# Queue orders of the mixing stage: sample scores at chunks 4 and 8, at mix's end and in retention, and queries times past states with sides swapped

## The chip, the cores and the metric

The kernel runs on 1 core of one Trainium2 chip. The metric is the device time of one execution in microseconds, and lower is better. A core has TensorE (PE in the profile), VectorE (DVE), ScalarE (ACT), GpSimd (POOL) and SyncE (SP), which here only issues DMAs. Engines are ordered among each other by semaphores alone; each runs its own instructions strictly in the order in which they are written.

## The reference, cut to what matters

The program is one inference step of a 2-layer decoder. Each layer has a feed-forward part, a mixing part and a second feed-forward part, over 256 prompt tokens and 8 sample sequences of 8 tokens each (320 columns in all).

```python
x = x + 0.5 * swiglu(rmsnorm(x, g_ffn1), f1_in, f1_out)
z = rmsnorm(x, g_mix) @ w_in
u, qa, ka, va, qr, kr, vr, gr = jnp.split(z, offs, axis=-1)
y_pool, pool_new = pool_mixer(u, pool_prefix, pos, pool_w, pool_scale)
y_att = ...   # per sequence: softmax over its own keys, and for samples over 8 cached pages of 128 keys
o_r, ret_new = retention(qr, kr * HEAD_DIM ** -0.5, vr, ret_s0)
y_ret = silu(gr) * o_r * rsqrt(mean(o_r ** 2) + EPS)
x = x + concat([y_pool, y_att, y_ret]) @ w_out
x = x + 0.5 * swiglu(rmsnorm(x, g_ffn2), f2_in, f2_out)
```

Retention of a sample adds the product of its queries, decayed, with its past state (a 64x64 matrix per head and sequence): `o = att @ v + (q * q_dec) @ s`.

## The kernel before

Every weight matrix streams from HBM in chunks of 256 columns (1 MB). SP loads a chunk into `w_raw` (two slots), ACT rounds it to `w_hi` (`hi_split`, L587), DVE forms the rest `w_lo` (`lo_split`, L844), and PE multiplies three times (L1235 to L1237 in the feed-forward parts, L1317 to L1319 in mixing). PE can start a chunk only when its `w_lo` is there.

The change lies in the mixing part of both layers, the body of the loop over `L` after the first feed-forward part. There each engine has an order of work that is written out by hand:

- PE runs `mix(0)` to `mix(11)`, the twelve chunks of `w_in`. `mix(c)` needs chunk c split and the first half of chunk c-1 evacuated (`evac_first(c-1)`, L933, which counts `mix_half`). Between chunks stand pieces of attention: `scores(f)` and `transpose_p(h)` and `att_out(f)` for the prompt; `sample_scores(p)` for pair p of the 8 sample sequences (p = 0 to 3); `past_states()`, the queries times the past states. Then come retention (`ret_scores`, `ret_out`, `smp_state`), the softmax results times the cached values (`smp_out`), and the output projection (`out_part`).
- `sample_scores(p)` multiplies the queries with 16 pages of keys: 8 pages in `kbuf[0]` and 8 in `kbuf[1]`. DVE must have turned them in place (`turn_k`, L990, half a buffer each). `key_scores` counts `sc_done` when it is done with a buffer.
- SP loads weight chunks (`mix_load(c)`) and pages (`next_k(p, bb)`: waits for `sc_done`, then issues 8 page loads of 192 KB). All these go through SP's one queue, in the order of the code. `mix_load(c)` also waits until chunk c-2 is split.
- DVE runs `evac_first`, `evac_last`, `mix_lo(c)` (a `lo_split`), `turn_k`, the prompt's softmax (`smax(h)`, `normalise(h)`), and the samples' (`soft_in(p)` reads the scores from PSUM, `soft_bias(p)` selects blocks and finds maxima, `soft_sum(p)` adds). ACT runs `mix_hi(c)` (a `hi_split`), the copies of turned tokens (`ka_tokens`, `va_tokens`), and the exponentials (`exp(h)`, `exps(p)`).
- POOL does the pooling sums, prepares queries (`qprep(p)`) and loads the pages of values (`load_v`).

Before the change `sample_scores(0)` stands ahead of `mix(6)`, (1) ahead of `mix(10)`, (2) after `ret_scores(1)` and (3) after the mean squares; SP has pages of pair 1 after chunk 8 and those of pair 2 after chunk 11. The scores of pair 3 use pair 0's buffer `sp_a` again.

`past_states` multiplies, for each of 3 pairs of heads, a stationary 128x128 block of states with 16 columns of queries at a time:

```python
pe.matmul(ps[:, 3, P * f + c:P * f + c + 2 * NT], s0[:, f, b:b + 2, :].rearrange("p b v -> p (b v)"),
          q[:, c:c + 2 * NT], start=True, stop=True)
```

Of the kernel before, what the change touches and what calls it, by code (L numbers as in the profile page):

```python
# [108 lines left out]
def build(nc, A, C, O):  # L109
# [8 lines left out]
    with ctx:  # L118
# [181 lines left out]
        def _(sp_e):  # L300
# [137 lines left out]
        def _(pool):  # L438
# [37 lines left out]
            with pool.Fori(0, DEPTH) as L:  # L476
# [26 lines left out]
                for n, w in enumerate(WINDOWS):  # L503
# [78 lines left out]
        def _(act):  # L582
# [63 lines left out]
            with act.Fori(0, DEPTH) as L:  # L646
# [20 lines left out]
                def va_tokens(t):  # L667
# [119 lines left out]
                act.wait_ge(stored_u, 32 * (L + 1))  # L787
                for f in range(3):
# [5 lines left out]
                exps(2)  # L794
# [921 lines left out]
```

## Time and profile before

| | us |
|---|---|
| median of 3 runs | 1453.36 (1450.92 to 1453.76) |
| the profiled execution's own time | 1445.9 |
| its span | 1443.9 |
| PE busy | 1360.1 (94%) |
| DVE busy | 812.1 (56%) |
| ACT busy | 650.0 (45%) |
| POOL busy | 216.7 (15%) |

The mixing part of the first layer lies between about 262 and 478 us of the span, that of the second between about 965 and 1179 us. In the trace a matmul's bar is longer than its share of the engine, since matmuls overlap; the distance from start to start tells what one takes. "[x <-Y]" at a row's end says that the engine was idle for x us before it, and what ended that.

### The profile page before, as it was taken

The numbers are of one execution on the slowest core, as the hardware profiler recorded it, in microseconds if no ns is written. First come the engines' busy times: TensorE is split into PE (matmuls) and PEld (weight loads), VectorE is DVE, ScalarE is ACT, GpSimd is POOL, SyncE is SP. The second block draws the span as 40 slices with busy tenths as digits, with TensorE's granted clock in tenths as the row PEclk, the third lists the DMA queues.
The fourth block names the chain that finished last, engine by engine and source line by source line (L and its number), as shares of the span: only waits on it lengthen the run. The fifth ranks groups of instructions, "written<-read, shape, count | busy, mean of one in ns | idle before, by whom it ended". The sixth has DMA issues, their size and how long they took to land.

```text
span 1443.9 us, 28417 instructions
## 1 busy us (share of the span) xinstructions
PE 1360.1 (94%) x11165; PEld 1306.2 (90%) x11165; DVE 812.1 (56%) x870; ACT 650.0 (45%) x715; POOL 216.7 (15%) x343
## 2 busy tenths in 40 slices
PE   6999999899877999999999999989997789999998
PEld 4999999899656899999999999989984579999998
DVE  4655545477673665554455555456867546555454
ACT  4655533334223565553355554432434245555433
POOL 3000001370334100000100000034313611000001
PEclk9999999999988999999999999999999899999998
DMA  6444445753758344444444444475637744444443
GB/s 207 150 145 145 143 160 180 209 166 115 219 179 277 118 145 146 151 152 144 152 142 156 152 145 135 158 236 142 208 110 221 258 153 146 145 145 145 142 153 121
DMA packets 210895, 235.27 MB, mean 163 GB/s; under 512 B 14974, under 2 KB 203144, under 8 KB 210804
## 3 DMA queue, kind: packets, MB, share of 16 engines
q1 hardware_dynamic: 200828, 204.90, 43.8%
q0 software_dynamic: 9856, 29.14, 6.4%
q8 instruction: 55, 0.90, 0.3%
q14 instruction: 36, 0.29, 0.1%
q10 hardware_dynamic: 120, 0.03, 0.0%
HBM read 228.83 MB, written 5.32 MB: 162 GB/s over the span
## 4 chain that ended last, share of the span: by engine, by line
PE 84%; issue 7%; DVE 5%; DVEq 1%; POOLq 1%; DMA 1%; ACT 1%; POOL 0%; SPq 0%; ACTq 0%
PE ps L1235 21%; PE ps L1237 21%; PE ps L1236 21%; PE ps L1317 4%; PE ps L1319 4%; PE ps L1318 4%; PE ps L1457 2%; DVE kbuf L990 1%; PE ps L1495 1%; PE ps L1402 1%; DVEq L1165 1%; PE ps L1630 1%; DVE h_lo L851 0%; DVE w_lo L844 0%; DMA x_tok<-in_x_sample 0%
## 5 line engine op out<-in xcount | busy, mean ns | idle before, releaser
L587 ACT ACTIVATE w_hi<-w_raw 128x2048 fp32r<-128x2048 f32 x170 | 325.6, 1915 | 554.6 <-PE ps L1237 427.3
L844 DVE TENSOR_TENSOR w_lo<-w_raw,w_hi 128x2048 fp32r<-128x2048 f32 x170 | 391.4, 2303 | 210.4 <-ACT w_hi L587 207.7
L1235 PE MATMUL ps<-h_hi,w_hi 128*128 128x320 f32 x768 | 241.0, 314 | 9.5 <-DVE w_lo L844 3.5
L1236 PE MATMUL ps<-h_lo,w_hi 128*128 128x320 f32 x768 | 239.7, 312 | 0.0
L1237 PE MATMUL ps<-h_hi,w_lo 128*128 128x320 f32 x768 | 239.5, 312 | 0.0
L1235 PE MATMUL ps<-g_hi,w_hi 128*128 128x320 f32 x704 | 218.4, 310 | 1.2 <-DVE g_lo L851 1.2
L1237 PE MATMUL ps<-g_hi,w_lo 128*128 128x320 f32 x704 | 217.7, 309 | 0.0
L1236 PE MATMUL ps<-g_lo,w_hi 128*128 128x320 f32 x704 | 217.7, 309 | 0.0
L1236 PE MATMUL ps<-act_lo,w_hi 128*128 128x320 f32 x704 | 217.5, 309 | 0.0
L1235 PE MATMUL ps<-act_hi,w_hi 128*128 128x320 f32 x704 | 217.5, 309 | 0.0
L1237 PE MATMUL ps<-act_hi,w_lo 128*128 128x320 f32 x704 | 217.5, 309 | 0.0
L1235 PEld LDWEIGHTS ps<-h_hi,w_hi 128*128 128x128 f32 x768 | 146.2, 190 | 11.4 <-issue 5.9
L1236 PEld LDWEIGHTS ps<-h_lo,w_hi 128*128 128x128 f32 x768 | 146.3, 191 | 0.2
L1237 PEld LDWEIGHTS ps<-h_hi,w_lo 128*128 128x128 f32 x768 | 146.3, 191 | 0.0
L1235 PEld LDWEIGHTS ps<-g_hi,w_hi 128*128 128x128 f32 x704 | 132.2, 188 | 1.9 <-DVE g_lo L851 1.7
L1236 PEld LDWEIGHTS ps<-g_lo,w_hi 128*128 128x128 f32 x704 | 132.2, 188 | 0.2
L1237 PEld LDWEIGHTS ps<-g_hi,w_lo 128*128 128x128 f32 x704 | 132.2, 188 | 0.0
L1236 PEld LDWEIGHTS ps<-act_lo,w_hi 128*128 128x128 f32 x704 | 132.2, 188 | 0.0
L1237 PEld LDWEIGHTS ps<-act_hi,w_lo 128*128 128x128 f32 x704 | 132.2, 188 | 0.0
L1235 PEld LDWEIGHTS ps<-act_hi,w_hi 128*128 128x128 f32 x704 | 132.2, 188 | 0.0
L1317 PE MATMUL ps<-h_hi,w_hi 128*128 128x320 f32 x368 | 119.2, 324 | 8.1 <-DVE z L933 6.9
L449 POOL COPY ssq<-tmp 128x640 f32<-128x640 f32 x7 | 8.0, 1147 | 751.9 <-ACT tmp L612 751.9
(275 smaller groups left out, 1923.4 us busy)
## 6 DMA issues: line engine op xcount, KB each, us to landing
w_raw<-in_ffn_w_in SPq DMA_DIRECT2D x90, 1024.0 KB, 5.1
w_raw<-in_ffn_w_out SPq DMA_DIRECT2D x32, 896.0 KB, 4.6
kbuf<-in_cache_k SPq DMA_DIRECT2D x128, 192.0 KB, 3.3
w_raw<-in_w_in SPq DMA_DIRECT2D x22, 1024.0 KB, 5.7
w_raw<-in_ffn_w_out SPq DMA_DIRECT2D x16, 1024.0 KB, 5.0
kbuf<-in_cache_v POOLq DMA_DIRECT2D x64, 192.0 KB, 4.4
w_raw<-in_w_out SPq DMA_DIRECT2D x8, 1024.0 KB, 7.5
v_c<-in_cache_v POOLq DMA_DIRECT2D x32, 192.0 KB, 3.4
```

Of the source, the lines that this page charges most:

```text
L587: act.activation(w_hi[:, slot, :], w_raw[:, slot, :], ACT.Copy).then_inc(hi_done, 1)
L844: dve.tensor_tensor(w_lo[:, slot, :], w_raw[:, slot, :], w_hi[:, slot, :].bitcast(F32), ALU.subtract).then_inc(split_done, 1)
L990: dve.transpose(keys, keys).then_inc(kt_ok, 1)
L1165: dve.drain()
L1235: pe.matmul(out, w_hi[:, slot, w], hi[:, k, :], start=(k == 0), stop=False)
L1236: pe.matmul(out, w_hi[:, slot, w], lo[:, k, :], start=False, stop=False)
L1237: ins = pe.matmul(out, w_lo[:, slot, w], hi[:, k, :], start=False, stop=(k == k_all - 1))
L1317: pe.matmul(out, w_hi[:, c % 2, w], h_hi[:, k, :], start=(k == 0), stop=False)
L1318: pe.matmul(out, w_hi[:, c % 2, w], h_lo[:, k, :], start=False, stop=False)
L1319: ins = pe.matmul(out, w_lo[:, c % 2, w], h_hi[:, k, :], start=False, stop=(k == KT - 1))
L1402: pe.matmul(ps[:, 3, P * f + c:P * f + c + 2 * NT], s0[:, f, b:b + 2, :].rearrange("p b v -> p (b v)"), q[:, c:c + 2 * NT], start=True, st ...
L1457: ins = pe.matmul(ps[32 * f:32 * f + 32, 2 + r, 0:256], q_sc[p][R, bb, f, a, j, :], kbuf[bb][R, :, c:c + 32], start=(bb == 0 and n == 0), ...
```

## The change

1. PE: `sample_scores(0)` moves ahead of `mix(5)`, `sample_scores(1)` ahead of `mix(9)`, `sample_scores(2)` ahead of the later tokens of retention, `sample_scores(3)` ahead of the last `smp_state`; `scores`, `transpose_p` and `tokens` move by about one chunk the other way. `out_part(0, early)` moves behind `smp_out(2, 1)`.
2. SP: pages of pair 1 are loaded ahead of chunk 7, those of pair 2 ahead of chunk 10.
3. DVE and ACT: their orders follow. `turn_k` of pair 0 starts at chunk 0.
4. A buffer of its own for the scores of pair 3 (`sp_d`, in `w_lo`'s first slot), so `mix_lo(12)` now waits for all transposes of probabilities.
5. `past_states`: queries are the stationary side (32 columns), states the moving side (128 columns): 12 matmuls a layer in place of 27 (three times nine). The result lies by query rows, and `ret_out` turns it with two matmuls per head in place of one.

```diff
@@ block.sync
-                for c in range(3, 8):
+                for c in range(3, 7):
                     mix_load(c)
+                next_k(1, 0)
+                next_k(1, 1)
+                mix_load(7)
                 sp_e.wait_ge(u_out, 2 * L + 2)
...
                 mix_load(8)
-                next_k(1, 0)
                 sp_e.wait_ge(ka_out, 3 * L + 2)
                 store_kv(0, "k", ka_tok, None, stored_k)
-                next_k(1, 1)
                 mix_load(9)
+                next_k(2, 0)
+                next_k(2, 1)
+                mix_load(10)
                 sp_e.wait_ge(va_out, 3 * L + 2)
                 store_kv(0, "v", va_tok, None, stored_va)
-                mix_load(10)
                 mix_load(11)
-                next_k(2, 0)
-                next_k(2, 1)
@@ block.scalar
                 mix_hi(7)
                 ka_tokens(1)
+                exps(0)
                 exp(0)
                 exp(1)
                 mix_hi(8)
                 va_tokens(0)
+                mix_hi(9)
+                va_tokens(1)
                 probs_out(0)
                 probs_out(1)
                 exp(2)
                 exp(3)
-                mix_hi(9)
-                va_tokens(1)
-                exps(0)
                 mix_hi(10)
                 att_evac(0)
+                exps(1)
+                mix_hi(11)
+                ka_tokens(2)
                 probs_out(2)
                 probs_out(3)
...
@@ block.vector
                 evac_first(4)
-                turn_k(0, 1, 0)
                 evac_last(4)
+                mix_lo(6)
+                soft_in(0)
+                evac_first(5)
+                soft_bias(0)
+                evac_last(5)
+                mix_lo(7)
                 smax(0)
                 dve.drain()
                 smax(1)
-                mix_lo(6)
-                evac_first(5)
...
-                evac_last(7)
+                evac_last(8)
+                mix_lo(10)
                 normalise(2)
                 normalise(3)
-                mix_lo(9)
                 soft_sum(0)
-                turn_k(1, 0, 0)
-                evac_first(8)
-                turn_k(1, 0, 1)
-                evac_last(8)
+                dve.wait_ge(pool_d, L + 1)
+                soft_in(1)
+                evac_first(9)
+                soft_bias(1)
+                evac_last(9)
+                mix_lo(11)
                 smax(4)
                 dve.drain()
                 smax(5)
-                mix_lo(10)
...
+                evac_first(10)
+                turn_k(2, 0, 0)
+                evac_last(10)
+                turn_k(2, 0, 1)
                 dve.wait_ge(past_done, L + 1)
...
                 y_rest(0)
                 for f in range(3):
                     or_lo(f)
+                y_rest(1)
+                dve.wait_ge(pt2_done, NB * L + 8)
                 mix_lo(12)
@@ block.tensor
                     for f in range(3):
                         q = q_dec[:, f, :, :, :].rearrange("p b a t -> p (b a t)")
-                        pe.matmul(ps[HD:P, 3, P * f:P * f + NT], s0[:, f, 0, :], q[:, 0:NT], start=True, stop=True)
-                        for b in range(NB - 1):
...
+                        for g in range(4):
+                            ins = pe.matmul(ps[32 * g:32 * g + 32, 3, P * f:P * f + P], q[:, 32 * g:32 * g + 32],
+                                            s0[:, f, 2 * g:2 * g + 2, :].rearrange("p b v -> p (b v)"), start=True, stop=True)
...
                 u_tokens()
-                scores(0)
                 tokens(ZKA, 0, 7).then_inc(ka_tr, 1)
+                pe.wait_ge(kown_ok, L + 1)
+                sample_scores(0)
                 mix(5)
...
                 tokens(ZKA, 1, 7).then_inc(ka_tr, 1)
+                wait_apart(pe, sm_in, L * 4 + 1)
+                scores(0)
                 mix(6)
...
                 tokens(ZVA, 0, 7).then_inc(va_tr, 1)
-                transpose_p(0)
-                transpose_p(1)
-                scores(1)
                 mix(7)
                 pe.wait_ge(va_out, 3 * L + 1)
                 tokens(ZVA, 1, 7).then_inc(va_tr, 1)
+                transpose_p(0)
+                transpose_p(1)
+                wait_apart(pe, s_max, H * L + 2)
+                scores(1)
                 mix(8)
                 pe.wait_ge(va_out, 3 * L + 2)
                 att_out(0)
...
+                pe.wait_ge(s_max, H * L + 4)
+                sample_scores(1)
                 mix(9)
                 wait_apart(pe, oa_out, 3 * L + 1)
                 tokens(ZKA, 2, 7).then_inc(ka_tr, 1)
+                transpose_p(2)
+                transpose_p(3)
+                scores(2)
+                past_states()
                 mix(10)
                 pe.wait_ge(ka_out, 3 * L + 3)
                 att_out(1)
+                wait_apart(pe, past_ok, L + 1)
+                tokens(ZVA, 2, 3).then_inc(va_tr, 1)
+                mix(11)
```

Three places of the new orders follow, as the built programs have them.

SP's queue at the load of chunk 7, before (chunks 6 and 7, then the stores of `u_tok`):

```order
L305 DMA w_raw<-in_w_in 128x8x256
L303 ISA
L305 ISA
L305 DMA w_raw<-in_w_in 128x8x256
L303 REGISTER_ALU
L305 ISA
L305 DMA w_raw<-in_w_in 128x8x256
L376 ISA
L377 ISA
L377 DMA out_pool_prompt<-u_tok 15x256
```

and after the change (the last page of the 16 of pair 1, then chunk 7; `kbuf_60` is `kbuf[1]`):

```order
L358 ISA
L358 DMA kbuf_60<-in_cache_k 128x384
L304 REGISTER_ALU
L306 ISA
L306 DMA w_raw<-in_w_in 128x8x256
L380 ISA
L381 ISA
L381 DMA out_pool_prompt<-u_tok 15x256
```

The 16 page loads of pair 1, which wait for the scores of pair 0, now stand ahead of chunk 7.

DVE at the split of chunk 7, before (`smax(0)`'s end and `smax(1)`, chunk 6, `evac_first(5)`, `turn_k`, `evac_last(5)`, chunk 7; L933 is `evac_first`, L938 `evac_last`):

```order
L949 SCALAR_TENSOR_TENSOR s_p<-dist_p,ps 128x384
L952 TENSOR_REDUCE st<-s_p 128x1
L953 TENSOR_REDUCE st<-s_p 128x1
L955 TENSOR_SCALAR st<-st 128x2
L843 ISA
L844 TENSOR_TENSOR w_lo<-w_raw,w_hi 128x2048
L932 REGISTER_ALU
L933 TENSOR_TENSOR z<-ps,rstd 128x320
L990 STREAM_TRANSPOSE kbuf_60<-kbuf_60 128x1536
L936 REGISTER_ALU
L938 TENSOR_TENSOR z<-ps,rstd 128x320
L843 REGISTER_ALU
```

and after (chunk 7's split L847, then `smax(0)` and `smax(1)`, then `evac_first(6)` L936):

```order
L847 TENSOR_TENSOR w_lo<-w_raw,w_hi 128x2048
L948 ISA
L952 SCALAR_TENSOR_TENSOR s_p<-dist_p,ps 128x384
L955 TENSOR_REDUCE st<-s_p 128x1
L956 TENSOR_REDUCE st<-s_p 128x1
L958 TENSOR_SCALAR st<-st 128x2
L948 REGISTER_ALU
L952 SCALAR_TENSOR_TENSOR s_p<-dist_p,ps 128x384
L955 TENSOR_REDUCE st<-s_p 128x1
L956 TENSOR_REDUCE st<-s_p 128x1
L958 TENSOR_SCALAR st<-st 128x2
L935 REGISTER_ALU
```

`smax(0)` and `smax(1)` stood ahead of the splits of chunks 6 and 7, and stand behind that of chunk 7 now, ahead of `evac_first(6)`.

DVE after `evac_first(8)`, after the change (the end of `q_dec`, `evac_last(8)`, chunk 10's split, `normalise(2)`, `normalise(3)`):

```order
L1098 TENSOR_TENSOR q_dec<-z,q_decay 64x8x8 x6
L939 REGISTER_ALU
L941 TENSOR_TENSOR z<-ps,rstd 128x320
L846 ISA
L847 TENSOR_TENSOR w_lo<-w_raw,w_hi 128x2048
L963 RECIPROCAL st<-st 128x2
L965 TENSOR_SCALAR s_p<-s_p,st 128x256
L966 TENSOR_SCALAR s_p<-s_p,st 128x128
L963 RECIPROCAL st<-st 128x2
L965 TENSOR_SCALAR s_p<-s_p,st 128x256
L966 TENSOR_SCALAR s_p<-s_p,st 128x128
```

Before, `normalise(2)` and `normalise(3)` followed `evac_last(7)` at once and stood ahead of chunk 9's split; now they stand behind chunk 10's.

## Rows read from the trace of the kernel before

**Rows 1.** Busy time by stretches: start:end, length, PE, PEld, DVE, ACT, POOL, PEclk, DMA share, GB/s

```profile
640.00:680.00 40.00, 40.00 (x275) 40.00 (x274) 19.45 (x14) 15.79 (x12) 1.21 (x1) 1.00 0.45 145
400.00:440.00 40.00, 25.18 (x401) 16.81 (x400) 28.43 (x56) 11.15 (x29) 17.39 (x36) 0.78 0.63 195
```

**Rows 2.** PE in order of time (start us, us), first layer: chunks 7, 8, 10, 11; the projection

```profile
325.06 0.42 PE L1317 MATMUL ps<-h_hi,w_hi 128*128 128x320 f32 x1
332.44 0.39 PE L1317 MATMUL ps<-h_hi,w_hi 128*128 128x320 f32 x1
365.64 0.41 PE L1317 MATMUL ps<-h_hi,w_hi 128*128 128x320 f32 x1
374.31 0.39 PE L1317 MATMUL ps<-h_hi,w_hi 128*128 128x320 f32 x1
...
439.19 0.65 PE L1503 MATMUL ps<-ident,o_tok 96*128 96x96 f32 x2 [7.35 <-ACT o_tok L720]
...
470.88 0.41 PE L1630 MATMUL ps<-h_hi,w_hi 128*128 128x320 f32 x1 [0.97 <-DVE h_lo L1177]
```

**Rows 3.** In order of time: the end of chunk 4 (DVE's last evacuation), the scores of pair 0 (PE)

```profile
302.39 0.49 DVE L938 TENSOR_TENSOR z<-ps,rstd 128x320 f32<-128x320 f32 x1 [0.47 <-PE ps L1319]
...
311.42 4.28 PE L1457 MATMUL ps<-kbuf,q_sc_a 32*32 32x256 f32 x192
```

**Rows 4.** SP's queue in order of time, first layer

```profile
314.61 5.04 SPq L357 DMA_DIRECT2D kbuf<-in_cache_k  x8
...
321.09 5.50 SPq L357 DMA_DIRECT2D kbuf<-in_cache_k  x8
326.84 0.38 SPq L305 DMA_DIRECT2D w_raw<-in_w_in  x1
...
362.99 10.46 SPq L357 DMA_DIRECT2D kbuf<-in_cache_k  x16
```

**Rows 5.** DMA issues of 326.8:327.3, then of 284:286: KB each, us to landing

```profile
w_raw<-in_w_in SPq DMA_DIRECT2D x1, 1024.0 KB, 7.8
...
w_raw<-in_w_in SPq DMA_DIRECT2D x1, 1024.0 KB, 5.3
```

**Rows 6.** The page's groups by line: the two halves of a split (busy us, mean ns)

```profile
L587 ACT ACTIVATE w_hi<-w_raw 128x2048 fp32r<-128x2048 f32 x170 | 325.6, 1915 | 554.6 <-PE ps L1237 427.3
L844 DVE TENSOR_TENSOR w_lo<-w_raw,w_hi 128x2048 fp32r<-128x2048 f32 x170 | 391.4, 2303 | 210.4 <-ACT w_hi L587 207.7
```

**Rows 7.** DVE in order of time: two `smax`; then `soft_in(0)`, `evac_first`, `soft_bias(0)`, `evac_last`

```profile
303.67 0.56 DVE L949 SCALAR_TENSOR_TENSOR s_p<-dist_p,ps 128x384 f32<-128x384 f32 x1 [0.79 <-PE ps L1367]
307.03 2.28 DVE L844 TENSOR_TENSOR w_lo<-w_raw,w_hi 128x2048 fp32r<-128x2048 f32 x1
...
317.79 1.22 DVE L997 TENSOR_REDUCE ss<-ps 96x4 f32<-96x1024 f32 x1 [0.18 <-issue]
320.63 0.49 DVE L933 TENSOR_TENSOR z<-ps,rstd 128x320 f32<-128x320 f32 x1 [0.17 <-issue]
...
324.56 0.48 DVE L938 TENSOR_TENSOR z<-ps,rstd 128x320 f32<-128x320 f32 x1
```

**Rows 8.** PE in order of time: `past_states` begins, chunk 9 begins behind it; a piece of `smp_out`

```profile
342.12 0.28 PE L1399 MATMUL ps<-q_dec,s 128*64 128x8 f32 x2
...
348.26 0.64 PE L1317 MATMUL ps<-h_hi,w_hi 128*128 128x320 f32 x1
...
453.64 1.95 PE L1495 MATMUL ps<-v_d,pt_s 128*32 128x128 f32 x48
```

**Rows 9.** Stretches, columns as in rows 1: chunk 9 behind `past_states`, PE around and after its longest wait

```profile
349.00:354.00 5.00, 5.00 (x20) 5.00 (x20) 1.98 (x2) 0.00 (x0) 0.00 (x0) 0.50 0.00 0
436.00:446.00 10.00, 5.60 (x68) 4.51 (x71) 5.17 (x8) 6.89 (x21) 6.85 (x13) 0.51 0.99 347
```

**Rows 10.** PE in order of time: the scores of pair 3, first and second buffer

```profile
416.49 3.56 PE L1457 MATMUL ps<-kbuf,tmp 32*32 32x256 f32 x96 [3.38 <-DVE kbuf L990]
422.43 3.84 PE L1457 MATMUL ps<-kbuf,tmp 32*32 32x256 f32 x96 [2.39 <-DVE kbuf L990]
```

More of the change, by code:

```diff
@@ L755, in _ @@
                 exp(5)
-                mix_hi(11)
-                ka_tokens(2)
+                att_evac(1)
                 va_tokens(2)
-                att_evac(1)
                 probs_out(4)
                 probs_out(5)
-                exps(1)
                 act.wait_ge(stored_va, 16 * (L + 1))
@@ L793, in _ @@
                     root_o(f)
-                exps(2)
                 probs_evac(0)
-                for f in range(3):
-                    or_high(f)
+                exps(3)
                 out_evac(0, 0)
@@ L800, in _ @@
                 probs_evac(1)
+                for f in range(3):
+                    or_high(f)
                 y_high(0)
-                exps(3)
-                mix_hi(12)
                 out_evac(1, 0)
@@ L1066, in _ @@
                 smax(1)
-                mix_lo(6)
-                evac_first(5)
-                turn_k(0, 1, 1)
-                evac_last(5)
-                mix_lo(7)
+                evac_first(6)
+                turn_k(1, 0, 0)
+                evac_last(6)
+                mix_lo(8)
                 normalise(0)
                 normalise(1)
-                soft_in(0)
-                evac_first(6)
-                soft_bias(0)
-                evac_last(6)
+                turn_k(1, 0, 1)
+                evac_first(7)
+                turn_k(1, 1, 0)
+                evac_last(7)
+                mix_lo(9)
+                turn_k(1, 1, 1)
                 smax(2)
@@ L1080, in _ @@
                 smax(3)
-                mix_lo(8)
-                evac_first(7)
+                evac_first(8)
                 dve.memset(q_dec[:], 0.0)
@@ L1104, in _ @@
                 smax(5)
[L1105 to L1109 removed]
+                evac_first(10)
+                turn_k(2, 0, 0)
+                evac_last(10)
+                turn_k(2, 0, 1)
                 dve.wait_ge(past_done, L + 1)
[L1111 to L1114 removed]
+                for half in range(2):
+                    ins = dve.tensor_copy(o_past[half][:], ps[:, 3, 0:384].rearrange("p (f b v) -> p f b v", f=3, b=2)[:, :, half, :])
                 ins.then_inc(past_ok, 1)
[L1116 removed]
                 normalise(4)
                 normalise(5)
[L1119 to L1125 removed]
+                evac_last(11)
+                turn_k(2, 1, 0)
+                turn_k(2, 1, 1)
+                soft_sum(1)
+                dve.wait_ge(chunk_used, L * C_ALL + (C_MIX + 14))
+                soft_in(2)
                 dve.wait_ge(stored_k, 32 * (L + 1))
@@ L1137, in _ @@
                 k_tokens(2)
-                turn_k(2, 1, 0)
-                turn_k(2, 1, 1)
                 decay_mask(1)
+                soft_bias(2)
+                turn_k(3, 0, 0)
                 for t in range(2):
@@ L1149, in _ @@
                 decay_mask(3)
+                turn_k(3, 0, 1)
                 gate(0)
-                soft_in(2)
+                decay_mask(4)
+                turn_k(3, 1, 0)
                 new_state(0)
-                decay_mask(4)
+                decay_mask(5)
+                turn_k(3, 1, 1)
                 gate(1)
                 new_state(1)
-                decay_mask(5)
                 gate(2)
+                soft_in(3)
                 new_state(2)
-                soft_sum(1)
-                soft_bias(2)
+                soft_sum(2)
+                soft_bias(3)
                 def or_norm(f):
@@ L1178, in y_rest @@
                     ins.then_inc(ys_low, 1)
-                for half in range(2):
-                    turn_k(3, 0, half)
-                or_norm(0)
-                for half in range(2):
-                    turn_k(3, 1, half)
-                soft_in(3)
-                soft_sum(2)
-                soft_bias(3)
-                or_norm(1)
-                or_norm(2)
+                for f in range(3):
+                    or_norm(f)
                 y_rest(0)
@@ L1647, in _ @@
                 transpose_out(2)
+                chunk_split(half0 + C_WO // 2, 0)
+                wait_apart(pe, o_std, 3 * L + 3)
+                pe.wait_ge(att_low, L + 1)
+                pe.wait_ge(ret_low, 3 * L + 3)
+                out_part(0, early, True)
                 smp_out(3, 0)
```

107 lines of the change are left out of this document (37 added, 70 removed).

## Prediction

> **What bounds the kernel now.** I read the table of busy time by stretches first, then PE in order of time through the mixing part of the first layer, then SP's queue and DVE's order at the places where PE would wait. In the feed-forward parts PE is busy for all of a 40 us stretch [rows 1], so the change can neither gain nor lose there. In the mixing part PE has holes: 25.2 of 40 us busy between 400 and 440, at a granted clock of 0.78 [rows 1]. The longest wait is 7.35 us, for ACT's `o_tok`, the longest of the waits for keys is 3.4 us [rows 2, 10]. Up to chunk 11, though, the chunks follow each other nearly without a hole, 7.4 us apiece (332.44 less 325.06) [rows 2]. So PE is the bound up to there, with DVE, ACT and the weight chunks ahead of it by some microseconds, and in the tail PE, DVE and ACT wait in turn. The same order of work runs in both layers; I work out one and double it.
>
> **The change part by part.**
>
> *Where pair 0 is scored.* Chunk 4 ends at 302.4 [rows 3]. Then come some 0.7 us of turned tokens and, now, `sample_scores(0)`. Its queries, its keys and its own keys are prepared in time: POOL's first pooling step now starts some 1 us after DVE's copy of the prefix and is followed by `qprep(0)`, and the four `turn_k` of 1.8 us each stand in places where DVE waited for PE. I take nothing for them; if they were late, the scores and all behind them would shift by as much as the 1.8 us of one `turn_k`. So the scores run from 303.1 to 307.7: 4.3 us, and 0.4 for the own keys [rows 3]. This is only a move; chunk 5 starts later and chunk 6 at about 316.4, as before within half a microsecond.
>
> *Chunk 7 behind 16 pages.* This is the term that decides. Half of the scores free `kbuf[0]`, at 305.3. In the trace SP's first page went out 1.0 us after that point (314.61 against 311.42 + 2.1) [rows 3, 4], so now at 306.3. Sixteen pages take SP 10.5 us to issue [rows 4]: 316.8. Chunk 7 is issued 0.3 us later, at 317.1. A chunk lands 5.3 us after its issue on an empty queue, and 7.8 behind 16 pages [rows 5]; I take 6.5, in the middle, with both as ends: 323.6. ACT's half of the split is 1.9 us and DVE's 2.3 [rows 6], with 0.1 for each hand-over: 327.9. Behind it on DVE stand `smax(0)` and `smax(1)`, 3.3 us together (303.67 to 307.03 [rows 7]), since the change put them behind the split, and only then `evac_first(6)`, 0.5, for which `mix(7)` waits: 331.7. PE is ready at 324.1 and idles for over 7 us. Chunk 7 started at 325.1 before [rows 2], so 6.6 us are lost (5.4 to 7.9 by the two landings).
>
> *To the scores of pair 1.* Chunk 7 is 7.4 us; its tokens, `transpose_p(0)`, `transpose_p(1)` and `scores(1)`, 2.0 in all, now follow it: `mix(8)` at 341.1, against 332.4 [rows 2]. It ends at 348.5, `att_out(0)` takes 0.8, and then PE waits for `smax(3)`, which I find at 350.2 by adding up DVE's order from `evac_first(6)` on. So `sample_scores(1)` begins at 350.2.
>
> *Chunk 10 behind 16 pages.* The same once more, and worse. `kbuf[0]` is free at 352.6, the pages go out from 353.0 to 363.5 [rows 4], chunk 10 at 363.8, landing at 370.3 (369.1 to 371.6) [rows 5], split at 374.7 [rows 6]. PE has done with chunk 9 at about 362.3 and then needs `att_evac(0)`, which stands behind `mix_hi(10)` on ACT, and `normalise(2)`, `normalise(3)` and `soft_in(1)`, which stand behind `mix_lo(10)` on DVE: 1.8, 0.4 for `soft_sum(0)`, and 2.8 (317.79 to 320.63 [rows 7]): 379.7. Then 0.4 for `transpose_p(3)`, 0.9 for `scores(2)`, and `past_states`: `mix(10)` begins at 382.0 against 365.6 [rows 2].
>
> *`past_states` with sides swapped.* Before, it takes 6.1 us (342.12 to 348.26) [rows 8] and leaves PE at the lower of its two clock levels: 0.50 of 2.4 GHz over 349 to 354, 20 records in 5 us [rows 9] where chunk 7 has 48 in 7.4, so 1.8 us lost in that stretch, 2.7 over all that runs slowly. The new form is nearest to `smp_out`, also 32 stationary and 128 moving columns: 48 records in 1.9 us [rows 8], 39 ns each. The 12 matmuls make 24 records, 0.9 us; even at the old 6.1 us it would be no loss. A gain of 5.2, 7.9 with the clock, is already in the 382.0 above. The extra matmul per head in `ret_out` adds under 0.2 us three times.
>
> The Trainium skill, TensorE: Matmul & The Clock Gate, section Back-to-back issue gap, puts a stream of weight loads and matmuls of 128 columns at about 81 ns each. By that `past_states` would take 1.9 us (an estimate from the page: 24 records), and the layer's sum would stay, since DVE sets the next step; the row's 39 ns speaks for less.
>
> *To chunk 11.* DVE goes on from 379.7: `evac_first(9)` 0.5, `soft_bias(1)` 3.6, `evac_last(9)` 0.4 (the last two by [rows 7]): 384.2. `mix_hi(11)` stands on ACT behind `exps(1)` (2.5): 388.6, `mix_lo(11)` 390.9, `smax(4)`, `smax(5)` 394.3, `evac_first(10)`, two `turn_k`, `evac_last(10)` 4.5: 398.8, and the copies of `o_past`, 0.7. The tokens that chunk 11 stands behind wait for these, since they use their bank. `mix(11)` begins at 399.9, against 374.3 [rows 2]: 25.6 us late.
>
> *The tail.* For: the waits of 3.4 and 2.4 us for the keys of pair 3 go [rows 10], since `sp_d` and the earlier place give these time. Against: `mix_lo(12)` may start only after the last transposes of probabilities, so its 2.3 us show ahead of `out_part(0)`; and `exps(3)`, `soft_bias(3)` and the three reciprocals now stand close together where PE waited 7.35 us [rows 2]. I find 2.5 us gained from `mix(11)` to the last parts of the projection; ends are 10 gained (both waits for keys and half of the 7.35) and 3 lost.
>
> *The clock.* PE's wait of 7.35 us was followed by the lower level: 0.51 over 436 to 446 [rows 9]. Three waits of 7, 16 and 9 us are new; the slow stretches after `past_states` and at the scores of pair 3 go. I take the two as equal, with 7 us more per layer as the upper end.
>
> *Sum.* 25.6 - 2.5 = 23.1 us per layer, some 46.5 in all. The profiled execution, 1445.9 us by its own time with a span of 1443.9, would be about 1492. The median of the runs stands 7.5 above it, so the median comes to 1453.4 + 46.6 = **1500 us**.
>
> **The rivals.**
>
> *Rival 1: the chunks are late, but the tail gives most of it back.* What is done later in the middle is done while the tail's other work catches up; the tail has some 20 us of idle PE and a low clock [rows 1, 2, 10]. Against it: the tail's waits are on DVE and ACT chains that cannot start before retention. It would leave some 8 to 12 us per layer: 1469 to 1477, say 1474.
>
> *Rival 2, the other side: the chunks are in time.* The kernel then gains. Place: chunk 7's and chunk 10's splits. It decides at 324 for chunk 7 and at about 364 for chunk 10: if pages and chunk together land 4 us sooner for the first, and 11 sooner for the second, PE never waits. Then `past_states` gives 7.9 us and the tail 2.5 to 4: 11 per layer, 1431. Against it stand the issue time of 16 pages, seen at 10.5 us without anything in between, and the landing of the chunk behind them [rows 4, 5].
>
> *Rival 3: the clock costs more.* Every long wait is followed by up to 8 us at 1.2 GHz, as after 439 [rows 2, 9], and none of it hides: 7 us more per layer, 1514. The Trainium skill, TensorE: Matmul & The Clock Gate, section What's actually happening, has the low clock as the default that only activity lifts; by it this rival holds at each of the three waits. Against it: after them DVE, not PE, sets the next step.
>
> *Rival 4: the change does not do what it says.* The fourth home lets `soft_in(3)` run early, but nobody waits for it if the values' pages or the reciprocals come last. It is inside the tail's range.
>
> **How the numbers follow.** Late chunks with the tail as worked out, 0.62 (1500, its own range 1486 to 1511); rival 3, 0.13 (1514); rival 1, 0.16 (1474); rival 2, 0.07 (1431); chunks partly late so that gain and loss cancel, 0.02. The range of 1470 to 1520 leaves out rival 2 and the edges of 1 and 3. A measurement of this kernel can tell about 0.2%, 3 us: faster 0.07, same 0.02, slower 0.91.
>
> **What would show it.** In the profile after: ACT's `w_hi` waits for the DMA of chunks 7 and 10; PE idles some 7 us ahead of chunk 7 and 16 in all ahead of chunk 10, and again ahead of chunk 11; `past_states` under 2 us; SP's `w_raw` issues behind 16 of `kbuf`. Wrong would be: chunk 7 starting by 326, or a distance of `mix(11)` to the projection's last parts that is shorter than 96.6 us (470.88 less 374.31 [rows 2]) by far more than 10.

## The result and the profile after

| | before | after |
|---|---|---|
| median of 4 runs, us | 1452.14 (1448.64 to 1453.76) | 1529.1 (1526.51 to 1531.54) |
| profiled execution, own time | 1445.9 | 1526.51 |
| its span | 1443.9 | 1524.5 |
| mean granted TensorE clock | 0.974 | 0.939 |

The ratio is 1.0538, with an interval of 1.0514 to 1.0562: 77 us slower, against 46.6 forecast. The direction and the mechanism of the late chunks hold; the tail's term does not, and the time lies above the forecast's range.

From the page of the profile after: PE's busy time, the shares of the chain that ended last, and DVE's half of a split [rows 6]:

```profile
PE 1382.4 (91%) x11129; PEld 1316.8 (86%) x11129; DVE 815.0 (53%) x870; ACT 653.6 (43%) x717; POOL 211.0 (14%) x343
PE 81%; DVE 6%; issue 3%; DMA 3%; SPq 3%; ACT 2%; DVEq 1%; POOLq 0%; POOL 0%; ACTq 0%
L847 DVE TENSOR_TENSOR w_lo<-w_raw,w_hi 128x2048 fp32r<-128x2048 f32 x170 | 389.6, 2292 | 286.5 <-ACT w_hi L589 263.0
```

DMA and SP's own queue now have 3% each of the chain (1% and 0% before); and DVE waits 263.0 us for ACT's `w_hi` ahead of its splits, 207.7 before [rows 6]. The split itself takes no longer (2292 ns, 2303 before). PE has 22 us more busy time with 36 fewer instructions, at a mean granted clock of 0.939 in place of 0.974.

Busy time by stretches (columns as in rows 1), first layer, cut at the stage's first evacuation, at `mix(11)` and at the late parts of the projection. Before:

```profile
270.90:374.30 103.40, 101.16 (x1056) 95.70 (x1057) 72.82 (x128) 32.33 (x61) 30.77 (x59) 0.95 0.51 153
374.30:470.90 96.60, 73.99 (x1128) 56.66 (x1126) 51.50 (x96) 32.62 (x84) 42.01 (x78) 0.88 0.70 224
```

After, with the stretches around the waits below them:

```profile
273.00:405.30 132.30, 100.31 (x1021) 92.23 (x1021) 75.21 (x127) 34.30 (x69) 28.21 (x59) 0.85 0.41 123
405.30:510.70 105.40, 83.20 (x1144) 63.82 (x1142) 50.73 (x98) 32.15 (x76) 42.00 (x78) 0.80 0.64 200
332.00:340.00 8.00, 3.44 (x13) 3.44 (x14) 6.81 (x13) 6.45 (x21) 0.00 (x0) 0.50 0.52 176
372.00:391.00 19.00, 6.15 (x43) 4.14 (x44) 10.07 (x27) 2.88 (x5) 0.00 (x0) 0.50 0.33 101
402.00:408.00 6.00, 3.22 (x13) 3.18 (x14) 3.96 (x11) 0.48 (x1) 0.00 (x0) 0.51 0.07 16
434.00:453.00 19.00, 17.55 (x135) 10.23 (x142) 12.16 (x23) 2.98 (x12) 4.07 (x4) 0.50 0.21 69
```

The second layer from `mix(11)` to the projection's late parts, before and after:

```profile
1075.40:1171.90 96.50, 71.38 (x1127) 55.19 (x1125) 51.42 (x96) 32.39 (x84) 41.99 (x78) 0.89 0.70 225
1144.07:1253.22 109.15, 88.90 (x1144) 68.08 (x1142) 50.84 (x98) 32.45 (x76) 42.00 (x78) 0.76 0.61 193
```

Two different losses stand here. Up to `mix(11)` the stage is 28.9 us longer and PE's busy time is nearly the same (101.2 and 100.3): idle time went from 2.2 to 32.0 us. From `mix(11)` to the projection, the tail, it is 8.8 us longer and the idle time is the same (22.6 and 22.2): PE is busy 9.2 us more, at a mean clock of 0.80 in place of 0.88. The second layer, cut at the same instructions, lost 28.2 and 12.6 us. In its tail PE idles 4.9 us less than before and is busy 17.5 us more, at 0.76 in place of 0.89. The first stage also began 2.1 us later in this execution; in the profiles of the kernels below its start lies anywhere from 269.7 to 273.0, whatever they change. From the stage's first matmul to that of the next part the layers lost 37.7 and 40.8, and 2.1 + 37.7 + 40.8 is the whole 80.6 us between the spans.

The first loss, chunk 7, is a piece of the chain of waits (start us, us, engine or queue, what, line; DVEq is DVE's sequencer, and L952 to L958 are `smax`):

```profile
319.93 8.39 DMA w_raw<-in_w_in
328.42 1.92 ACT w_hi L589
330.50 2.62 DVEq L954
...
334.21 0.55 DVE s_p L952
...
336.01 0.50 DVE z L936
336.56 0.63 PE ps L1316
```

and DVE's half of the split, then PE, in order of time:

```profile
330.36 2.29 DVE L847 TENSOR_TENSOR w_lo<-w_raw,w_hi 128x2048 fp32r<-128x2048 f32 x1 [9.62 <-ACT w_hi L589]
...
330.85 0.88 PE L1359 MATMUL ps<-ident,z 128*128 128x128 f32 x3 [3.59 <-ACT ka_tok L667]
336.56 0.63 PE L1316 MATMUL ps<-h_hi,w_hi 128*128 128x320 f32 x1 [4.83 <-DVE z L936]
```

Ahead of these rows the chain runs through SP's page issues. The forecast's steps follow each other as it named them: the chunk's transfer, ACT's half, DVE's half, the two `smax`, `evac_first(6)`, `mix(7)`. PE idles 8.4 us ahead of chunk 7, the first 3.6 of them for ACT's copy of `ka_tok`, which stands behind `mix_hi(7)`. Chunks 10 and 11, in order of time (answers to rows 2, 4 and 8):

```profile
358.69 10.49 SPq L358 DMA_DIRECT2D kbuf<-in_cache_k  x16
369.48 0.38 SPq L306 DMA_DIRECT2D w_raw<-in_w_in  x1
377.53 1.91 ACT L589 ACTIVATE w_hi<-w_raw 128x2048 fp32r<-128x2048 f32 x1 [21.77 <-DMA w_raw<-in_w_in]
379.47 2.29 DVE L847 TENSOR_TENSOR w_lo<-w_raw,w_hi 128x2048 fp32r<-128x2048 f32 x1 [22.29 <-ACT w_hi L589]
379.86 0.82 PE L1359 MATMUL ps<-ident,z 128*64 128x128 f32 x3 [11.56 <-ACT z L695]
388.95 1.51 PE L1399 MATMUL ps<-s,q_dec 128*32 128x128 f32 x24
390.38 0.64 PE L1316 MATMUL ps<-h_hi,w_hi 128*128 128x320 f32 x1
...
404.78 0.82 PE L1359 MATMUL ps<-ident,z 128*64 128x128 f32 x3 [5.63 <-DVE o_past L1122]
```

ACT stood still for 21.8 us and DVE for 22.3 while SP issued pages and the chunk flew. PE idled 16.6 us in three waits ahead of chunk 10 (11.56; 1.85 for the normalised probabilities; 3.14 whose end the profile puts down to no engine), and 5.6 ahead of chunk 11. `past_states` takes 1.5 us at the lower clock level. The two chunks' transfers, issue to landing (answers to rows 5):

```profile
w_raw<-in_w_in SPq DMA_DIRECT2D x1, 1024.0 KB, 8.4
...
w_raw<-in_w_in SPq DMA_DIRECT2D x1, 1024.0 KB, 7.9
```

PE's waits in the tail:

```profile
423.09 2.79 PE L1359 MATMUL ps<-ident,z 128*128 128x128 f32 x12 [4.33 <-DVE kr_tok L972]
435.45 0.69 PE L1421 MATMUL ps<-vr_tok,kr_tok 128*64 128x64 f32 x8 [4.92 <-DVE h_lo L1147]
...
460.08 3.50 PE L1519 MATMUL ps<-o_sq,head_mean 128*128 128x320 f32 x6 [1.87 <-DVE sp_d L1006]
...
486.99 3.26 PE L1495 MATMUL ps<-v_c,pt_s 128*32 128x128 f32 x48 [2.63 <-DMA v_c<-in_cache_v]
494.47 0.61 PE L1629 MATMUL ps<-h_hi,w_hi 128*128 128x320 f32 x1 [2.57 <-DVE w_lo L847]
```

The old waits for keys and the 7.35 us for `o_tok` [rows 2, 10] are gone. In their place stand two waits for DVE at retention's start, and behind the second the granted clock is 0.50 for all of 434 to 453: retention's matmuls run there at 1.2 GHz.

### The profile page after: what moved, and what is told of

It is laid out like the page before. It is cut to its first block, busy times and chain, and to the rows that moved or that the text cites. A ratio compares the mean times of both kernels' runs of the same rounds, so it can differ in the third digit from the quotient of the medians.

```text
span 1524.5 us, 28343 instructions
## 1 busy us (share of the span) xinstructions
PE 1382.4 (91%) x11129; PEld 1316.8 (86%) x11129; DVE 815.0 (53%) x870; ACT 653.6 (43%) x717; POOL 211.0 (14%) x343
## 4 chain that ended last, share of the span: by engine, by line
PE 81%; DVE 6%; issue 3%; DMA 3%; SPq 3%; ACT 2%; DVEq 1%; POOLq 0%; POOL 0%; ACTq 0%
PE ps L1234 21%; PE ps L1235 21%; PE ps L1236 21%; PE ps L1316 3%; PE ps L1317 2%; PE ps L1318 2%; DMA w_raw<-in_w_in 2%; SPq L358 2%; PE ps L1457 2%; PE ps L1495 2%; DVE w_lo L847 1%; ACT w_hi L589 1%; DVE h_lo L854 1%; PE ps L1629 1%; DVEq L954 1%
## 5 line engine op out<-in xcount | busy, mean ns | idle before, releaser
L847 DVE TENSOR_TENSOR w_lo<-w_raw,w_hi 128x2048 fp32r<-128x2048 f32 x170 | 389.6, 2292 | 286.5 <-ACT w_hi L589 263.0
L1235 PE MATMUL ps<-h_lo,w_hi 128*128 128x320 f32 x768 | 239.2, 311 | 0.0
L1234 PEld LDWEIGHTS ps<-g_hi,w_hi 128*128 128x128 f32 x704 | 132.3, 188 | 1.9 <-DVE g_lo L854 1.7
L1235 PEld LDWEIGHTS ps<-g_lo,w_hi 128*128 128x128 f32 x704 | 132.3, 188 | 0.2
L1236 PEld LDWEIGHTS ps<-g_hi,w_lo 128*128 128x128 f32 x704 | 132.3, 188 | 0.0
L1317 PE MATMUL ps<-h_lo,w_hi 128*128 128x320 f32 x368 | 118.9, 323 | 0.0
```

The source lines that it names most:

```text
L847: dve.tensor_tensor(w_lo[:, slot, :], w_raw[:, slot, :], w_hi[:, slot, :].bitcast(F32), ALU.subtract).then_inc(split_done, 1)
L1234: pe.matmul(out, w_hi[:, slot, w], hi[:, k, :], start=(k == 0), stop=False)
L1235: pe.matmul(out, w_hi[:, slot, w], lo[:, k, :], start=False, stop=False)
L1236: ins = pe.matmul(out, w_lo[:, slot, w], hi[:, k, :], start=False, stop=(k == k_all - 1))
L1317: pe.matmul(out, w_hi[:, c % 2, w], h_lo[:, k, :], start=False, stop=False)
```

## The experiments

Theory Q: the loss is SP's order, nothing else of the change. Rival D: the new orders of PE, ACT and DVE lose by themselves. Then each part of what was left was taken up in turn. "Against before" is the ratio to the kernel before, run on the same chip between them; where gains are compared below, it is by these ratios, since the median of before moved by up to 6 us from one group of runs to the next. The last columns are layer 1's two stretches in the profile, stage start to `mix(11)` and from there to the projection's late parts.

| kernel | median, us | against before | to mix(11) | tail |
|---|---|---|---|---|
| before | | 1 | 103.4 | 96.6 |
| the change | 1529.1 | 1.0538 [1.0514, 1.0562] | 132.3 | 105.4 |
| e2: chunk 7 ahead of the pages | 1509.89 | 1.0412 [1.0386, 1.0438] | 123.9 | 107.1 |
| e3: chunk 10 ahead | 1491.33 | 1.0297 [1.0270, 1.0325] | 116.3 | 105.3 |
| e1: both ahead | 1476.27 | 1.0196 [1.0169, 1.0223] | 105.6 | 107.0 |
| e5: e1, DVE's tail order | 1464.47 | 1.0117 [1.0094, 1.0139] | 106.4 | 101.4 |
| e6: e1, chunk 11 ahead too | 1465.48 | 1.0128 [1.0103, 1.0152] | 100.8 | 108.0 |
| e7: the change, SP's order of before | 1460.05 | 1.0093 [1.0070, 1.0116] | 99.3 | 107.1 |
| e9: e7, DVE's tail order | 1448.7 | 1.0002 [0.9987, 1.0018] | 100.2 | 99.9 |
| e10: e9, ACT's order, early copies | 1436.69 | 0.9918 [0.9890, 0.9946] | 94.7 | 99.1 |
| e11: e10, spread first | 1433.71 | 0.9896 [0.9873, 0.9918] | 95.6 | 97.8 |
| e12: e11, unit 5 before 4 | 1433.27 | 0.9909 [0.9882, 0.9936] | 95.1 | 95.8 |
| e4: before, swap alone | 1439.83 | 0.9936 [0.9914, 0.9959] | 97.9 | 99.4 |
| e8: e4, early copies | 1434.25 | 0.9903 [0.9880, 0.9926] | 94.1 | 99.1 |

**SP's queue: e1, e2, e3.** The edits, on the change; e2 has the first alone, e3 the second:

```diff
-                for c in range(3, 7):
+                for c in range(3, 8):
                     mix_load(c)
                 next_k(1, 0)
                 next_k(1, 1)
-                mix_load(7)
...
+                mix_load(10)
                 next_k(2, 0)
                 next_k(2, 1)
-                mix_load(10)
```

> The changed kernel with chunk 7 loaded ahead of pair 1's pages and chunk 10 ahead of pair 2's, nothing else. Theory Q (the queue): PE's waits of 8 us ahead of chunk 7 and of 16 us ahead of chunk 10 are the late landings, and the low clock behind them; both go, chunk 7 begins within 2 us of its old distance from the stage's start, and 20 to 28 us per layer come back: 1473 to 1489 us. Rival D (the orders of DVE and ACT cost as much by themselves): PE waits at the same places for softmax pieces, under 10 us per layer come back: over 1509 us.

> Only chunk 7 ahead of pair 1's pages. Theory Q: 6 to 10 us per layer come back, 1509 to 1517 us, and PE's wait ahead of chunk 10 stays. Rival D: under 3 us per layer, since smax(0) and smax(1) stand ahead of evac_first(6) anyway: over 1523 us.

> Only chunk 10 ahead of pair 2's pages. Theory Q: 12 to 18 us per layer come back, 1493 to 1505 us; with e2's the two returns add up to e1's within 4 us. Rival D: under 5 us per layer: over 1519 us.

Two lines moved bring back 50 of 78 us, and e1's median lies within theory Q's range; chunk 7 alone gives 18 and chunk 10 alone 35, which add up to 53. e2 lies within its range; e3 gave more than expected (1491.33 against 1493 to 1505). What is left, in e1's trace:

```profile
363.01 1.91 ACT L588 ACTIVATE w_hi<-w_raw 128x2048 fp32r<-128x2048 f32 x1 [4.31 <-DMA w_raw<-in_w_in]
...
364.95 2.29 DVE L846 TENSOR_TENSOR w_lo<-w_raw,w_hi 128x2048 fp32r<-128x2048 f32 x1 [8.31 <-ACT w_hi L588]
...
375.19 0.82 PE L1358 MATMUL ps<-ident,z 128*64 128x128 f32 x3 [8.13 <-DVE o_past L1121]
...
394.15 2.53 PE L1358 MATMUL ps<-ident,z 128*128 128x128 f32 x12 [4.33 <-DVE kr_tok L971]
...
406.89 0.70 PE L1420 MATMUL ps<-vr_tok,kr_tok 128*64 128x64 f32 x8 [5.04 <-DVE h_lo L1146]
```

The tail's two waits are as long as with late chunks (4.33 and 4.92 there), so they are no echo of the late chunks. And chunk 11 has a lateness of its own.

**Chunk 11, and the old queue: e6, e7.** e6 puts `mix_load(11)` ahead of pair 2's pages as well; e7 takes SP's whole order from the kernel before (the first piece of the change's diff, undone).

```diff
                 mix_load(10)
+                mix_load(11)
                 next_k(2, 0)
                 next_k(2, 1)
                 sp_e.wait_ge(va_out, 3 * L + 2)
                 store_kv(0, "v", va_tok, None, stored_va)
-                mix_load(11)
```

> Edit, made on the kernel with both chunks ahead of the pages (1476.27 us): chunk 11's load too stands ahead of pair 2's 16 pages, so its issue moves from 357.43 to about 348 and ACT and DVE split it some 8 us earlier. Theory C (the 8.13 us wait ahead of the value tokens and chunk 11 is DVE standing at chunk 11's split with o_past's copies queued behind): the wait falls to under 2 us, 6 us a layer come back, 1464, range 1459 to 1468. Rival P (pair 2's pages and the store of the values come later by 2 us, and the wait moves to the turned keys of pair 2 or to stored values): 1470 to 1477.

> Edit: the changed kernel with the whole order of SP's queue as before the change (chunk 7, the stores and chunk 8 ahead of pair 1's first pages; chunks 10 and 11 ahead of pair 2's). Theory N (the new order of PE and DVE needs pair 1's pages early, since DVE's turn_k(1,0,0) stands ahead of evac_last(6) and mix_lo(8)): chunks 7 and 10 are in time, but DVE waits some 5 us for the pages, mix(8) and what follows are 3 to 5 us later than with both chunks ahead of the pages: 1484, range 1477 to 1494. Rival O (the pages are in time where they were; the reordering of the queue was needless): 1462 to 1476.

e6: theory C. The wait ahead of chunk 11 falls from 8.13 to 4.00, not under 2, with the median in the range. e7: rival O, and better than its range; I had expected the pages of pair 1 to be late for DVE. e7's trace:

```profile
308.07 5.24 SPq L358 DMA_DIRECT2D kbuf<-in_cache_k  x8
318.38 5.96 SPq L358 DMA_DIRECT2D kbuf<-in_cache_k  x8
...
356.66 1.90 ACT L588 ACTIVATE w_hi<-w_raw 128x2048 fp32r<-128x2048 f32 x1
358.59 2.29 DVE L846 TENSOR_TENSOR w_lo<-w_raw,w_hi 128x2048 fp32r<-128x2048 f32 x1 [3.89 <-ACT w_hi L588]
...
368.83 0.53 PE L1358 MATMUL ps<-ident,z 128*64 128x128 f32 x3 [4.00 <-DVE o_past L1121]
```

The pages of pair 1 go out as two batches of 8, 10 us apart, and no wait of PE or DVE for them shows. So the new order of SP bought nothing, and by the ratios it cost 64 of the 78 us; the other 13 are rival D's. What is left ahead of chunk 11 is ACT: the chunk has long landed, but `exps(1)` stands ahead of `mix_hi(11)`.

**DVE in the tail: e5, e9.** The same edit on e1 and on e7:

```diff
-                dve.wait_ge(chunk_used, L * C_ALL + (C_MIX + 14))
-                soft_in(2)
                 dve.wait_ge(stored_k, 32 * (L + 1))
                 decay_mask(0)
...
                 k_tokens(2)
                 decay_mask(1)
-                soft_bias(2)
-                turn_k(3, 0, 0)
+                dve.wait_ge(chunk_used, L * C_ALL + (C_MIX + 14))
+                soft_in(2)
...
                 decay_mask(3)
+                soft_bias(2)
+                turn_k(3, 0, 0)
                 turn_k(3, 0, 1)
```

> Edit, made on the kernel with both weight chunks ahead of the pages (1476.27 us): in the retention part DVE does decay_mask(0), k_tokens(0) to (2) and decay_mask(1) first, then soft_in(2), and soft_bias(2) with turn_k(3,0,0) only after decay_mask(3). Theory T (the forecast's tail term failed because DVE's softmax work of pair 2 now stands ahead of what PE waits for there): both waits of that kernel's trace, 4.33 us on kr_tok and 5.04 us on h_lo, shrink by at least 5 us together in each layer, the other waits of the tail stay: 1466, range 1460 to 1470. Rival V (behind the retention part the tail is set by the value pages, which POOL issues 8 at a time, so what is won ahead of them is lost at the wait for v_c, 3.09 us before): under 2 us a layer, 1472 to 1478.

> Edit: the changed kernel with SP's queue as before the change (that alone 1460.05 us) and with the three moves of DVE's softmax work of pair 2 (soft_in(2), soft_bias(2), turn_k(3,0,0) behind the key tokens and masks). If the queue and the tail order are two separate losses, they add: 1460.05 less the 11.8 us that the tail moves gave beside the other queue (1476.27 to 1464.47) makes 1448, range 1445 to 1452. Rival: the page issues of the later part bound it from somewhere, and the moves give under half: 1454 to 1460.

Theory T, twice: 11.4 us by the ratios on e1 and 13.2 on e7. With e9 the change stands even with the kernel before. Most of it is idle time: PE idles 4.1 and 4.4 us less in the two layers' tails in e5 than in e1, and 4.6 and 4.3 less in e9 than in e7. In e5's trace one wait, which the expectation did not have, took the place of the two:

```profile
398.35 0.45 PE L1420 MATMUL ps<-vr_tok,kr_tok 128*64 128x64 f32 x8 [0.89 <-DVE h_lo L1144]
405.22 1.12 PE L1444 MATMUL ps<-tmp,kr_tok 64*64 64x512 f32 x2 [4.38 <-POOL tmp L540]
...
400.55 2.45 POOL L546 DMA_DIRECT2D v_c<-in_cache_v  x4 [0.57 <-issue]
```

POOL issues four value pages ahead of `spread_v`, which PE now waits for.

**ACT, the copies, POOL: e10, e11, e12.** e10 on e9, e11 on e10, e12 on e11, one after the other. In e10 the same copies of `o_past` behind `turn_k(2, 0, 1)` go:

```diff
-                exps(1)
                 mix_hi(11)
+                exps(1)
...
                 mix_lo(11)
+                dve.wait_ge(past_done, L + 1)
+                for half in range(2):
+                    ins = dve.tensor_copy(o_past[half][:], ...)
+                ins.then_inc(past_ok, 1)
                 smax(4)
```

```diff
-                wait_apart(pool, att_low, L + 1)
-                load_v(0, 0)
                 pool.wait_ge(vr_out, 3 * L + 3)
                 spread_v(0)
                 spread_v(1)
+                wait_apart(pool, att_low, L + 1)
+                load_v(0, 0)
```

```diff
+                wait_apart(pool, pv_done, NB * L + 1)
+                load_v_all(5)
                 wait_apart(pool, pt2_done, NB * L + 4)
                 load_v_all(4)
-                for u, n in ((5, 1), (6, 3), (7, 4)):
+                for u, n in ((6, 3), (7, 4)):
```

> Edit, made on the one just described: ACT splits chunk 11 (mix_hi(11)) ahead of exps(1) as against behind it, and DVE copies o_past directly behind mix_lo(11), ahead of smax(4) and smax(5). Theory A (the 4.00 us wait ahead of the value tokens that is left in mix with the old queue is ACT at exps(1) and DVE's smax, turns and copies behind it): the wait goes, 3 to 4 us a layer, 1441, range 1438 to 1444 if the one before gives 1448; that is 6 to 8 us below it. Rival: exps(1) later makes soft_sum(1) or the transposes of pair 1 late, under 3 us in all.

> Edit, made on the one just described: POOL does spread_v(0) and (1) ahead of the four value pages of load_v(0,0). Theory S (the 4.38 us wait for POOL's tmp that took the place of the waits for DVE is the page issues ahead of spread_v): 2 to 4 us a layer less than the one before, so 4 to 8 us. Rival (the retention part waits next for DVE's masks, or the end is set by the page issues after sample_scores(3), whose number is the same): under 2 us in all. Below 1434.25 us it would also beat the kernel before with the swap and the early copies.

> Edit, made on the kernel of the last run (1433.71 us): POOL issues the eight value pages of unit 5 (into v_c) ahead of those of unit 4 (into v_d), since POOL stands idle 5.19 us at unit 4's transposes while unit 5's home is already free. Theory I (the 3.18 us wait for v_c is POOL's issue order): that wait goes, unit 4's pages land some 1.3 us later and cost part of it back at their own product; 1 to 2 us a layer, 1431, range 1429 to 1433. Rival H (unit 4's pages, now issued last, are late by as much as unit 5's were): 1433 to 1437.

e10 gave 12 us (6 to 8 expected, so its median lies below its range): the wait of 4 us is gone in each layer, and so is the slow start of chunk 11 behind it (its start is at full clock now). e11 gave 3 us, between its two expectations and within what the intervals leave open, though its wait did shrink, from 4.85 to 1.18 in layer 1 and from 5.38 to 2.00 in layer 2, where a wait of 3.25 for ACT's `o_sq` came up. e12 gave nothing that the medians show. e11, then e12:

```profile
390.17 1.97 PE L1444 MATMUL ps<-tmp,kr_tok 64*64 64x512 f32 x4 [1.18 <-POOL tmp L540]
441.73 3.36 PE L1494 MATMUL ps<-v_c,pt_s 128*32 128x128 f32 x48 [3.18 <-DMA v_c<-in_cache_v]
```

```profile
435.04 3.25 PE L1496 MATMUL ps<-v_d,pt_s 128*32 128x128 f32 x48 [4.17 <-DMA v_d<-in_cache_v]
```

The wait for `v_c` became one for `v_d`: which unit's pages go last decides only where the wait stands. That is rival H.

**The swap alone: e4, e8.** e4 is the kernel before with the new `past_states`, its copies and its use in `ret_out`; e8 moves the wait for `past_done` and the copies up, from behind `evac_last(9)`. e4 on before (nine matmuls per pair of heads become four, with the queries stationary), then e8 on e4:

```diff
-                        pe.matmul(ps[HD:P, 3, P * f:P * f + NT], s0[:, f, 0, :], q[:, 0:NT], start=True, stop=True)
...
+                        for g in range(4):
+                            ins = pe.matmul(ps[32 * g:32 * g + 32, 3, P * f:P * f + P], q[:, 32 * g:32 * g + 32],
+                                            s0[:, f, 2 * g:2 * g + 2, :].rearrange("p b v -> p (b v)"), start=True, stop=True)
```

```diff
                 mix_lo(10)
+                dve.wait_ge(past_done, L + 1)
+                for half in range(2):
+                    ins = dve.tensor_copy(o_past[half][:], ...)
+                ins.then_inc(past_ok, 1)
                 turn_k(1, 1, 0)
                 evac_first(9)
                 turn_k(1, 1, 1)
                 evac_last(9)
```

> The kernel before with past_states, o_past and ret_out of the change, all orders as before. If the swapped product is worth what the trace of before says (6.1 us less some 1.5, and no low clock behind it), 5 to 7 us per layer: 1438 to 1442 us. If the low clock had another cause or DVE takes the place: 1446 to 1452 us.

> Edit, made on the kernel before plus the swapped past states alone (1439.83 us): DVE copies o_past directly after mix_lo(10), ahead of turn_k(1,1,0), evac_first(9), turn_k(1,1,1), evac_last(9). Theory W (the 3.28 us wait ahead of sample_scores(1) is for these copies alone): PE starts the scores 3 us earlier, 1434, range 1431 to 1437. Rival K (the wait goes over to the turned keys, which end only 0.4 us ahead of the copies, since the copies' 0.6 us now stand ahead of them): 1438 to 1442.

```profile
341.44 0.86 PE L1398 MATMUL ps<-s,q_dec 128*32 128x128 f32 x24
...
353.47 5.71 PE L1456 MATMUL ps<-kbuf,tmp 32*32 32x256 f32 x192 [3.28 <-DVE o_past L1112]
```

```profile
341.76 0.86 PE L1398 MATMUL ps<-s,q_dec 128*32 128x128 f32 x24
...
353.37 1.02 PE L1456 MATMUL ps<-kbuf,tmp 32*32 32x256 f32 x30 [0.57 <-DVE kbuf L990]
```

The first fence is e4's trace, the second e8's. Both medians lie in their ranges. Counted from the stage's first matmul, PE was ready for the scores 8.0 us sooner in e4 and then waited 3.3 us for DVE's copies, for which it had waited 1.1 before; so the scores began 5.9 us sooner. With the copies ahead of the turned keys that wait is gone, and 0.6 us for the turned keys is left. e8, e10, e11 and e12 beat the kernel before by 0.8 to 1.0% and cannot be told apart; e8 does it with the old order of everything else.

## Why the prediction was wrong in size

*Mechanism and sign*: right for the late chunks, which are most of the loss. Both chunks queue behind 16 pages, ACT and DVE wait for the DMA, PE waits ahead of chunks 7, 10 and 11 (8.4, 16.6 and 5.6 us; some 7 and 16 were named for the first two); e1 to e3 and e7 show it by taking it away. The sum has a slip of its own: twice 23.1 is 46.2, not 46.6, which changes nothing.

*Up to mix(11)*: forecast 25.6, measured 28.9. "I take 6.5, in the middle" for the landing was 8.4 and 7.9; even the upper end of 7.8 was below. That 7.8 stood behind two batches of 8 pages with a store between them [rows 4], not behind 16 in a row. With the stage's later start taken off (2.1), `mix(7)` began 2.8 us after the forecast's 331.7, of which 1.9 is the landing. SP's 10.5 us for 16 pages and DVE's two `smax` came as forecast. At ACT's split of chunk 10 the lag had grown to 5.1 us (375.4 against 370.3). From the end of DVE's split of chunk 10 to `mix(11)` it took 23.5 us, not 25.2, and 3.3 remained.

*The tail, the step that failed*: "2.5 us gained", ends 10 gained and 3 lost; measured 8.8 and 12.6 lost. The waits for keys did go. What I left out is what `sample_scores(2)` brings with it in its new place: `soft_in(2)` ahead of `k_tokens(0)`, `soft_bias(2)` and a `turn_k` ahead of `h_lo`, on the engine that retention waits for. I had read PE's new order there and not DVE's. e5 and e9 put a price of 5.6 to 7.2 us per layer on it. That is about half of the miss of 11.3 and 15.1 us. With it mended, in e9, PE idles 18.0 us in each tail, 4.6 and 7.2 less than before: the idle time that the forecast saw going did go. But the tail is still 3.3 us longer than before in both layers, since PE is busy 7.8 and 10.4 us more there. That second half stands beside a lower granted clock. The 2.6 us of `mix_lo(12)` show ahead of `out_part(0)` as forecast (2.3).

*The clock, the other term that failed*: "I take the two as equal" held up to `mix(11)` and fell in the tail. Up to `mix(11)` PE is busy for 3.4, 6.2 and 3.2 us at the lower level around the three waits, half of which, 6.4 us, is loss; e7, with PE's same order and no late chunks, is busy 92.7 us there against 100.3, a loss of 7.6. The forecast's 7.9 us that the swap takes off pays for it, and before it was 101.2. In the tail PE is busy longer at a lower mean clock: 0.80 and 0.76 in the two layers in place of 0.88 and 0.89, and 0.81 and 0.80 in e9. Not all of it is owed to the new orders: e8's tail, whose order is that of before but for one matmul more per head in `ret_out`, also takes 99.1 us against 96.6 (99.7 against 96.5 in the second layer), at 0.84 and 0.83. Why the clock falls at one place and not at another stays open; no run here varied it alone.

*The rivals.* Rival 1 (the tail gives back) was the wrong way round. Rival 3 (the clock costs more), with its 1514, was nearest, and had the right direction: PE's busy time grew by 8.4 us in the first layer's stage and by 15.6 in the second's. Its place was wrong: the three waits did cost clock, but the swap pays for that, and the growth is all in the tail. Rival 2 (chunks in time) could be priced: e7 and e9 have them in time and stand at +13 and 0 us, not at 22 gained, since the tail and ACT's order had to be mended as well. Its "`past_states` gives 7.9 us" per layer is 4.6 alone and 7.0 with early copies (e4, e8).

*`past_states` itself*: forecast 0.9 us by `smp_out`'s 39 ns a record; measured 0.86 at full clock, 36 ns. The Trainium skill, TensorE: Matmul & The Clock Gate, section Back-to-back issue gap, has about 81 ns for a pair with 128 moving columns and no row for a stationary side as narrow as this one; the trace of this form, with 32 stationary columns, shows that the figure does not carry over to it, and the measurement decides.

## What to carry to other kernels

A queue is in order: before moving a load in it, add up what now stands ahead of the next one that somebody waits for (16 page loads took 10.5 us). When work moves on one engine, read the others' new orders at the place where it arrives: here the expected gain of the moved scores turned into two waits for DVE. Then look at the granted clock of each stretch beside its idle time: in the tail the idle time did not grow, and the loss stood in the busy time. And a faster step only pays when what follows it on the other engines is moved up too: the swap gave 9 us, and one more moved copy made it 14.

## What the runs showed of the hardware

A DVE instruction of `soft_bias` on 4 or 5 columns takes 0.13 to 0.29 us in the profile of before, but where `soft_bias(2)` meets POOL's `spread_v` one of its steps takes 2.0 to 2.9 us: in every profile of a kernel with the change's retention part but e12's (in e11's in the second layer alone), and in none of before, e4 and e8. From e1, DVE, then POOL:

```profile
401.32 0.23 DVE L1022 TENSOR_SCALAR ss<-ss 96x4 f32<-96x4 f32 x1
401.62 2.49 DVE L1024 TENSOR_TENSOR ss<-ss 96x5 f32<-96x5 f32 x1
...
402.03 2.05 POOL L540 TENSOR_TENSOR tmp<-vr_tok,own_b 64x512 f32<-64x512 f32 x2
```

It ends together with POOL's operation (404.11 and 404.08). The Trainium skill, SBUF — State Buffer, section SBUF: two separate sides, has the port pair that VectorE and GpSimd share as an exclusive lock held for a whole instruction, so that the loser waits; by it a VectorE operation with two inputs in SBUF, as this one, can lose it. The rows agree in that DVE waits, 2.3 us for a 0.16 us operation. They show more than one instruction's wait: DVE's operation began at 401.62, when POOL was still issuing its last page load (to 402.02), and ended only with the second of POOL's two operations. It lies ahead of `h_lo`, for which PE waited 5.04 us; what it alone costs was not tried.

Granted clock 0.50 was seen over 434 to 453 with PE busy for 17.55 of 19 us: once low behind a wait of 4.9 us, it stayed low through retention.

A 1 MB chunk issued behind 16 pages landed after 8.4 and 7.9 us; in e7, behind 8 pages that followed 8 others after a pause of 5 us, the one issued at 324.59 took 6.0.
